# Dilated attention run three units deep: a third score buffer, scores two units ahead, weight copies one unit later

## What is computed

```python
def odd_mixer(h, w_in, w_out):
    cq, ck, cv, sq, sk, sv = split_cols(h @ w_in, ODD_SPLITS)
    o_dil = dilated_attention(groups(cq), groups(ck), groups(cv), slopes)
    o_sb = stick_breaking_attention(...)
    return jnp.concatenate([heads_last(o_dil), heads_last(o_sb)], axis=-1) @ w_out

def dilated_attention(q, k, v, slopes):
    # per block of 128 queries, per group g with window w and dilation dil
    s = (einsum('bhqd,bhqnd->bhqn', q_g, k_g) * scale - slopes[g] * steps)   # steps 0, dil, ... w
    s = where(valid, s, -inf)
    m = max(s); e = exp(s - m); den = sum(e)
    o = einsum('bhqn,bhqnd->bhqd', e / den, v_g);  lse = m + log(den)
    ...
    wts = softmax(stack(lses, axis=0), axis=0)
    o = einsum('gbhq,gbhqd->bhqd', wts, stack(outs, axis=0))
```

## Time and profile before

| what | value |
|---|---|
| median of three runs | 2013.02 us (2012.4 to 2014.24) |
| span of the profiled execution, first to last instruction | 2012.9 us |
| instructions in it | 23881 |
| TensorE busy, matmuls | 1949.9 us |
| VectorE busy, ScalarE busy | 917.9 us, 727.6 us |
| mean granted TensorE clock | 0.992 of full |

### The profile page before, as it was taken

One profiled execution on the slowest core, in us unless ns is written; L12 is line 12 of the kernel. 1 busy time (PEld: TensorE's weight loads), 2 busy tenths in 40 slices (PEclk: granted clock), 3 DMA queues, 4 the chain that ended last, 5 costly groups with the idle time before them and its releaser, 6 DMA issues.

```text
span 2012.9 us, 23881 instructions
## 1 busy us (share of the span) xinstructions
PE 1949.9 (97%) x9847; PEld 1336.4 (66%) x9847; DVE 917.9 (46%) x1487; ACT 727.6 (36%) x1205; POOL 13.9 (1%) x28
## 2 busy tenths in 40 slices
PE   6999999999999899999999999999998999999999
PEld 4756743333333267767788887877787678888787
DVE  4365322221111145474466665335555456666533
ACT  4365211111111041585333333235343653333323
POOL 1000000000000000000000000000000000000000
PEclk8999999999999999999999999999999999999999
DMA  9458379999999951400233332222212023332311
GB/s 327 140 197 265 146 296 428 428 427 428 428 427 427 428 169 32 147 1 22 63 105 105 85 104 86 103 84 63 84 63 64 20 64 93 97 103 86 105 63 42
DMA packets 167166, 344.41 MB, mean 171 GB/s; under 512 B 19755, under 2 KB 142235, under 8 KB 151571
## 3 DMA queue, kind: packets, MB, share of 16 engines
q1 hardware_dynamic: 165907, 340.91, 46.4%
q0 software_dynamic: 944, 1.91, 0.4%
q10 hardware_dynamic: 208, 0.07, 0.0%
HBM read 340.76 MB, written 2.11 MB: 170 GB/s over the span
## 4 chain that ended last, share of the span: by engine, by line
PE 87%; DMA 7%; DVE 3%; ACT 2%; issue 1%; SPq 0%; DVEq 0%; ACTq 0%
PE bank L2116 22%; PE bank L1353 13%; PE bank L2133 12%; PE bank L1930 10%; PE bank L1949 4%; PE bank L1303 2%; PE bank L889 2%; DMA norm_area<-in_w_down 2%; DMA moe_high<-in_w_up 2%; DMA work<-in_w_up 2%; PE bank L910 2%; PE bank L1291 2%; PE bank L933 2%; DMA ring<-in_w_in 1%; PE bank L1899 1%; PE bank L1961 1%
## 5 line engine op out<-in xcount | busy, mean ns | idle before, releaser
L559 DVE TENSOR_TENSOR ring_low<-ring,w_high 128x2048 fp32r<-128x2048 f32 (+1 forms) x91 | 207.7, 2282 | 125.5 <-ACT w_high L552 125.4
L552 ACT ACTIVATE w_high<-ring 128x2048 fp32r<-128x2048 f32 x90 | 171.3, 1905 | 218.4 <-PE bank L2116 174.0
L2116 PE MATMUL bank<-h_high,ring_low 128*128 128x512 f32 x640 | 249.7, 390 | 0.0
L2116 PE MATMUL bank<-low_ff,w_high 128*128 128x512 f32 x608 | 238.3, 392 | 0.0
L2116 PE MATMUL bank<-h_high,w_high 128*128 128x512 f32 x608 | 236.5, 389 | 0.0
L2133 PE MATMUL bank<-ff_split,w_high 128*128 128x512 f32 x704 | 222.1, 395 | 1.6 <-DVE work L2840 1.6
L2133 PEld LDWEIGHTS bank<-ff_split,w_high 128*128 128x128 f32 x704 | 132.0, 188 | 36.2 <-DVE work L2840 2.4
L2133 PE MATMUL bank<-ff_split,ring_low 128*128 128x512 f32 x352 | 139.0, 395 | 0.0
L2116 PEld LDWEIGHTS bank<-h_high,ring_low 128*128 128x128 f32 x640 | 120.3, 188 | 26.5
L2116 PEld LDWEIGHTS bank<-h_high,w_high 128*128 128x128 f32 x608 | 114.1, 188 | 25.2
L2116 PEld LDWEIGHTS bank<-low_ff,w_high 128*128 128x128 f32 x608 | 114.1, 188 | 24.5
(11 more groups left out here) (459 smaller groups left out, 3394.4 us busy)
## 6 DMA issues: line engine op xcount, KB each, us to landing
ring<-in_ffn_w_up SPq DMA_DIRECT2D x88, 512.0 KB, 5.1
ring<-in_w_gate SPq DMA_DIRECT2D x16, 2048.0 KB, 23.0
ring<-in_w_down SPq DMA_DIRECT2D x12, 2048.0 KB, 27.0
ring<-in_ffn_w_down SPq DMA_DIRECT2D x22, 1024.0 KB, 4.7
ring<-in_w_ada SPq DMA_DIRECT2D x18, 1024.0 KB, 7.4
const<-in_w_gate SPq DMA_DIRECT2D x8, 2048.0 KB, 23.0
work<-in_w_up SPq DMA_DIRECT2D x8, 2048.0 KB, 22.9
ring<-in_w_up SPq DMA_DIRECT2D x8, 2048.0 KB, 23.5
```

Of the source, the lines that this page charges most:

```text
L552: act.activation(high_of(n, words), slab_view(g)[:, 0:words], ACT.Copy).then_inc(sem("split_high"), 1)
L559: dve.tensor_tensor(ring_low[:, slot_of(g), 0:words], slab_view(g)[:, 0:words], high_of(n, words).bitcast(F32), ALU.subtract).then_inc(sem ...
L2116: mm = pe.matmul(bank[n % 6][:, :], st[k], mv[k], start=(k == 0), stop=(k == len(st) - 1))
```

## The change

A third score buffer is laid over the masks (2560 columns of `const` from `MASKS` on). The three are reached through a small class, since they no longer lie in one array. `DIL_A` gets `ahead` = 2 in place of 1 and `copy_own` = False in place of True. Line numbers of the changed kernel are higher by 1 up to L755 and by 11 in what the prediction speaks of in the attention (L889 becomes L900).

```diff
-        s3 = a.take(2, 2, DIL_W)
+        s3_work = a.take(2, 2, DIL_W)
+        s3_masks = const[:, MASKS:MASKS + 2 * DIL_W].rearrange("p (r w) -> p r w", r=2)
...
+        class HeadRows:
+
+            def __init__(self, bufs):
+                self.bufs, self.shape = bufs, (P, len(bufs))
+
+            def __getitem__(self, key):
+                p, b, r, t = key
+                return self.bufs[b][r][p, t]
...
-        DIL_A = Attention(dil_units, HD ** -0.5, s3, pt3, [6, 7], 1, EVEN_A, True, scaled_bias=True)
+        s3 = HeadRows([[v[:, r, :] for r in range(2)] for v in (s3_work[:, 0], s3_work[:, 1], s3_masks)])
+        DIL_A = Attention(dil_units, HD ** -0.5, s3, pt3, [6, 7], 2, EVEN_A, False, scaled_bias=True)
```

## The result

| | before | changed |
|---|---|---|
| median (range), executions on the same chip | 2013.63 us (2012.4 to 2015.69), 4 | 2025.21 us (2022.46 to 2026.68), 4 |
| ratio of changed to before, 95% interval | | 1.0057 (1.0044 to 1.0069) |
| the profiled execution | span 2012.9 us | 2022.46 us, span 2020.7 us |

The changed kernel is slower by 11.6 us.

A forecast was written before the change was run, and what follows sets the result against it. No single engine bounds the dilated-attention stage, but a chain passing between engines. Waits of +7.6 and clock of +3.0 make +10.6 us on the 2012.9 us span: 2023.6 us, with an 8-in-10 range of 2017.5 to 2028.5.

The forecast's parts named there:

- the signs named ahead: Profile after: stage 8 to 12 us longer, same busy counts, VectorE idle about 11 us, a late turn waiting 2.9 us.
- Sum of the waits, +7.6: Dilated attention: longer PE waits at units 2 to 7 and at the stage's end add 7.6 us.
- unit 3: Wait before its third score group, behind weight copies and slab: 2.1 to 2.2 us, was 1.06, so +1.0.
- less 1.35 for two groups: At unit 3, PE's first two score groups cover 1.35 us of the 3.8 us chain.
- The drain, +2.3: Unit 6's third turn waits 2.9 us for a copy behind unit 7's exponentials; was 0.56, so +2.3.
- The third buffer, 0: Third score buffer removes a VectorE wait for turns that never showed in the trace: by itself worth 0.
- the copies beside P and S, 0: Mid-stage, with weights copied later, ScalarE's exponentials lie beside PE's values and scores and cost nothing.
- What holds the reads: VectorE's late output starts only when PE's values end, holding the next score reads; chain 3.4 us for unit 4.
- The clock, +3.0: Two more falls to 1.2 GHz after the new waits, 1.5 us each: +3.0 us, bounds 0 and +6.
- Every long wait drops the clock: Rival: each new long wait in the stage costs a clock fall; +13.6 us, 2026.6 us, chance 0.14.
- Faster: Rival: scores come early, waits of units 3 to 7 go; -4.8 us, 2008.2 us, chance 0.06.
- nothing much: Rival: waits before third score groups only change their name; +3.5 us, 2016.5 us, chance 0.08.

The follow-up runs named there:

- the repeat: The changed kernel run again, unaltered, beside the kernel before on the same chip: 2026.1 us, ratio 1.0054.
- both repairs: Changed kernel with VectorE's extra part behind the score reads and ScalarE copying unit 6 before unit 7's exponentials: 2012.56 us, ratio 0.9991.
- both edits: Kernel before with VectorE's extra part behind the reads and PE's third score group between the previous unit's second and third turn: 2009.04 us, ratio 0.9970.

## Why the prediction was right

The forecast was +10.6 us, 2023.6; the runs gave +11.6 and +12.3, and the place and the mechanism are the forecast's. The total is nearer than its two terms, and that is luck: the waits were put 1.6 us too high, and the clock, for the repeat's median execution, some 2.6 us too low. Of the signs named ahead, the busy counts, the waits behind VectorE (10.1 us, about 11 forecast), L579 directly behind L1075 and the 2.9 us at the drain all came; the stage grew by 7.7 us in one profile and 11.9 in the other, where 8 to 12 were forecast.

- **Sum of the waits, +7.6.** Measured +6.0 in the change's profile. Unit by unit, forecast and measured: unit 4, 2.5 and 2.35; unit 5, 1.6 to 1.7 and 1.78; unit 6, 1.2 and 1.24; unit 7, 0.8 and 0.71; unit 2, 2.06 plus 0.4 and 1.50 + 0.52 + 0.34 = 2.36. The one miss is **unit 3**, 2.1 to 2.2 forecast and 1.18 measured. The step that failed is "less 1.35 for two groups": they ran at half speed and took longer. With the clock up the same wait was 2.25, as the forecast has it. The other half microsecond of the gap lies in the other turns, those of units 1, 2 and 7, which wait 0.5 us less in all than they did (4.6 less 2.8 is 1.8, of which the drain alone makes 2.4). The forecast put them at 0.
- **The drain, +2.3.** Forecast 2.9, measured 2.92, released by the copy that was named; taking it away gave back 2.25 us of wait. The ratio went from 1.0054 to 1.0037, some 3.4 us; the intervals overlap, the ten times behind them do not.
- **The third buffer, 0; the copies beside P and S, 0.** The first is shown by its run. The second holds only with the scores two ahead; with the scores one unit ahead it costs 18.5 us.
- **What holds the reads.** The forecast put the late output first and said that "everything behind it in VectorE's queue" starts after it. The runs order the two: moving the late output alone changes nothing (1.0053 against 1.0054), moving the extra part alone takes the ratio to 1.0009. The chain's pieces were all in the sum, so its length came out nearly right: from L983 to PE's third group 2.95 us for unit 4 and 3.23 for unit 5, where the forecast had 3.4 and 3.2. One reading behind it was wrong without harm: L972 at 1559.41 doesn't stand at the end of a value product. Unit 0's values had ended at 1553.4, and it starts directly behind unit 2's copies. As a guide to a repair, the emphasis on L1075 would have misled. VectorE passed nothing by: in the run with the late output moved, reads whose scores were there stood behind a difference that waited 4.51 us. By the Trainium skill, "TensorE: Matmul & The Clock Gate", section on the array's detail, ScalarE's and VectorE's queues are strict first in, first out. The traces agree: for VectorE by this difference of 4.51 us, for ScalarE by L1003, which stood behind the copies until 1557.63 with its values there since 1552.0.
- **The clock, +3.0.** The number of falls differs between executions of the same instructions with the same waits. The profiled execution of the change had 3.4 us more at half clock than before (+1.4 at 0.41), its repeat 13.7 us more (+5.6). Added to 6.0, these give 7.4 and 11.6, against stages that grew by 7.7 and 11.9. The median lies with the second. The price of one fall, 1.5, was right (3.4 us at 0.41 is 1.4); the number of falls was the guess. Two falls more at 1.5 lie between the two profiles; what the forecast gave as one number is a spread. (Its own upper bound of +12 is too low for its terms: 7.6 and 6 are 13.6.) The four executions show it: spans of 2020.7 and 2022.9 us at a mean clock of 0.992, 2023.9 and 2024.9 at 0.990. The 0.41 comes from the same two profiles; runs that it was not taken from bear it out within 0.7 us. All columns are against the kernel before, for the stage, in us; the fourth is the second plus 0.41 of the third:

| run | PE's waits | at half clock | worked out | stage |
|---|---|---|---|---|
| late output one step later | +6.0 | +10.2 | +10.2 | +10.6 |
| extra part behind the reads | +1.9 | -3.4 | +0.5 | +0.7 |
| copies first at the end | +4.9 | +6.8 | +7.7 | +7.9 |
| copies later alone | +9.6 | +27.3 | +20.8 | +20.5 |
| both repairs | -0.4 | -3.4 | -1.8 | -1.5 |
| values ahead of the third group | +0.6 | +3.4 | +2.0 | +2.7 |

- **The rivals.** "Every long wait drops the clock", at 2026.6, is a little nearer to the two medians (2025.21 and 2026.1) than the forecast of 2023.6. Its rule is not what happens, though: in the repeat the clock fell after the waits of 1.51, 2.36 and 2.92 us and not after the one of 1.78 us; in the first profile it fell after 1.50 and 2.35 and not after 2.92. The Trainium skill, in "TensorE: Matmul & The Clock Gate", section on psum-queue depth-cycling, says that frequent short idle times between groups of matmuls make the clock swing between its two levels. The traces agree in direction (two and three falls where one was), but neither execution pays in every unit, as the forecast took it to mean: from unit 5 to the drain's wait the clock is at 1.00 in both. "Faster" fell with the chain at 2.9 us and more, "nothing much" with the units' waits at nearly their full forecast size.

## What to carry to other kernels

Deepening a software pipeline on engines with fixed queues changes which producer stands directly ahead of each consumer. For every instruction that now finishes late, list what stands behind it in each queue, and put side work (here the next stage's weights) behind the reads that another engine is waiting for. Count the drain apart: an order that hides copies behind the next unit's exponentials has no next unit at the end. Before adding depth, try the order of the side work in the shallow kernel: in this kernel that one line was worth 4 us and the depth nothing. And before a repair is called proof of a cause, look at the order of time after it: moving the values took the waits away without starting the chain any earlier.

## What the runs showed of the hardware

- The same instructions with the same waits had the clock at 1.2 GHz for 6.8 us of this stage in one execution and 17.1 in another, and differ by 4.2 us. For a kernel with idle stretches of some 2 us between dense work, one profile doesn't fix what the clock costs.
- A microsecond at half clock cost 0.41 us here, not 0.5, an estimate from two profiles that six other runs bear out within 0.7 us of stage time. At unit 3 the half-speed matmuls also shortened the wait that follows, from 2.25 to 1.2 us.
- Waits of 2.9 us didn't always drop it (the drain, in the change's first profile and in the run with the extra part behind the reads), while in the kernel before with both edits it fell at 1546.4 us, after two waits of only 0.98 and 1.18 us.
